# Two of nine tiles take their second expert table as one ordered pass and products with an on-chip weight matrix

## What is computed

```python
idx = jnp.take_along_axis(cidx, sel, axis=-1)      # cidx = i1 * 128 + i2
g = jax.nn.softmax(best, axis=-1)
ue = jnp.take(u, idx, axis=0)
ve = jnp.take(v, idx, axis=0)
a = jax.nn.gelu(jnp.einsum("thkd,td->thk", ue, tb), approximate=False)
return jnp.einsum("thk,thkd->td", g * a, ve)
```

## Time and profile before

| | before |
|---|---|
| median of 3 runs | 4154.73 us (4143.67 to 4164.61) |
| span of the profiled execution, first to last instruction | 4055.0 us |
| TensorE (PE) busy | 2755.5 us, 68% |
| VectorE (DVE) busy | 2362.3 us, 58% |
| GpSimd (POOL) busy | 2392.4 us, 59% |
| ScalarE (ACT) busy | 853.5 us, 21% |
| moved by DMA | 1373.95 MB, of it 1107.43 MB by the gathers |

### The profile page before, as it was taken

How to read it: one execution, slowest core, us unless ns; L and a number is a source line. 1 busy time by engine, 2 the same in 40 slices (tenths; PEclk the granted TensorE clock), 3 DMA queues, 4 the chain that set the end, 5 groups by cost and what they waited for, 6 DMA issues and landing times.

```text
span 4055.0 us, 39016 instructions
## 1 busy us (share of the span) xinstructions
PE 2755.5 (68%) x12071; PEld 1452.6 (36%) x12071; DVE 2362.3 (58%) x6192; ACT 853.5 (21%) x1884; POOL 2392.4 (59%) x2148
## 2 busy tenths in 40 slices
PE   8989987877789975568787888987453332333334
PEld 5667564534445432234444444443121000000000
DVE  2134356578865556646488886654566666666552
ACT  1235212244421110112144442111010000000000
POOL 1000034667756547756477776654777777777775
PEclk9989988977779987779877778998776665566556
DMA  6443387999999989989999999997999999999998
GB/s 219 124 142 101 139 285 268 389 359 385 390 349 394 386 336 375 395 312 387 356 387 361 385 394 394 381 374 289 368 391 388 381 370 367 385 387 366 382 369 345
DMA packets 540797, 1373.95 MB, mean 339 GB/s; under 512 B 50640, under 2 KB 246800, under 8 KB 540592
## 3 DMA queue, kind: packets, MB, share of 16 engines
q0 software_dynamic: 304128, 1107.43, 71.4%
q1 hardware_dynamic: 195040, 220.24, 16.2%
q10 hardware_dynamic: 41424, 43.80, 3.3%
HBM read 1319.26 MB, written 52.02 MB: 338 GB/s over the span
## 4 chain that ended last, share of the span: by engine, by line
PE 33%; POOL 25%; DMA 13%; DVE 11%; issue 10%; DVEq 3%; ACT 2%; SPq 1%; ACTq 1%; PEldq 0%; POOLq 0%; PEld 0%
POOL G_v_rows L713 13%; POOL G_u_rows L713 12%; PE scores L837 7%; DMA G_v_rows<-in_peer_v,G_idxT 5%; PE scores L1721 5%; PE y_sum L2226 4%; PE scores L1725 3%; DVE G_u_rows L2060 3%; PE scores L1915 3%; PE scores L1503 3%; PE scores L1810 2%; DMA scratch_dkT<-A_dkT 2%; PE scores L1410 2%; PE o L1445 1%; DMA D_w_br<-in_w_br_m 1%
## 5 line engine op out<-in xcount | busy, mean ns | idle before, releaser
L713 POOL DMA_INDIRECT G_u_rows<-in_peer_u,G_idx x1056 | 1199.9, 1136 | 756.7 <-issue 321.8
L2060 DVE CUSTOM_DVE_ANT_0 G_u_rows<-G_u_rows,G_h 128x1024 f32<-128x1024 f32 x1056 | 1274.7, 1221 | 431.2 <-DMA G_u_rows<-in_peer_u,G_idx 408.4
L713 POOL DMA_INDIRECT G_v_rows<-in_peer_v,G_idxT x1056 | 1177.9, 1115 | 486.9 <-issue 312.4
L2226 PE MATMUL y_sum<-G_v_rows,G_zw 128*32 128x512 f32 x4224 | 749.7, 846 | 877.1 <-DMA G_v_rows<-in_peer_v,G_idxT 853.0
L2226 PEld LDWEIGHTS y_sum<-G_v_rows,G_zw 128*32 128x32 f32 x4224 | 148.9, 137 | 1358.5 <-issue 1354.6
L837 PE MATMUL scores<-A_w_in,A_hT 128*128 128x256 f32 (+2 forms) x864 | 221.9, 417 | 22.9 <-DMA A_w_in<-in_w_in 15.5
L668 POOL MEMSET G_zw<- 128x1024 f32 x2 | 1.9, 963 | 395.9 <-SPq L630 395.9
L837 PEld LDWEIGHTS scores<-A_w_in,A_hT 128*128 128x128 f32 x864 | 168.7, 198 | 74.8 <-DMA A_w_in<-in_w_in 16.4
L1721 PE MATMUL scores<-D_hT,D_w_gate 128*128 128x384 f32 x512 | 172.9, 491 | 2.3 <-DMA D_w_br<-in_w_br_m 2.1
L1428 PE MATMUL turn<-ident,C_probs 128*128 128x128 f32 x635 | 133.4, 327 | 49.1 <-ACT C_pT L1536 41.2
L1960 DVE COPY F_sc<-scores 128x256 f32<-128x256 f32 (+1 forms) x72 | 29.3, 422 | 215.2 <-PE scores L1926 215.1
(11 more groups left out here) (282 smaller groups left out, 3940.7 us busy)
## 6 DMA issues: line engine op xcount, KB each, us to landing
A_w_in<-in_w_in SPq DMA_DIRECT2D x24, 1024.0 KB, 13.3
D_w_gate<-in_w_gate SPq DMA_DIRECT2D x24, 1024.0 KB, 22.9
G_u_rows<-in_peer_u,G_idx POOLq DMA_INDIRECT x1056, 7.8
G_v_rows<-in_peer_v,G_idxT POOLq DMA_INDIRECT x1056, 8.2
DF_w<-in_w_gate SPq DMA_DIRECT2D x12, 1024.0 KB, 21.0
DF_w<-in_peer_wq SPq DMA_DIRECT2D x12, 1024.0 KB, 10.3
F_w_q<-in_peer_wq SPq DMA_DIRECT2D x12, 1024.0 KB, 7.1
E_w_o<-in_w_o SPq DMA_DIRECT2D x18, 512.0 KB, 8.5
```

Of the source, the lines that this page charges most:

```text
L713: pool.indirect_dma_start(out=buf[:, :], out_offset=None, in_=table, in_offset=bass.IndirectOffsetOnAxis(ap=rows, axis=0)).then_inc(signal ...
L2060: dve.tensor_tensor_reduce(out=self.u_rows[slot][:, :], in0=self.u_rows[slot][:, :], in1=self.h2[t % 2][:, :], scale=1.0, scalar=0.0, op0= ...
L2226: last = pe.matmul(self.ps_y[32 * c:32 * (c + 1), cols], self.zw[b % 2][:, lo:lo + 32], self.v_rows[self.ring_v.slot[4 * quad + c]][:, col ...
```

## The change

For the token tiles 4 and 5 (places 5 and 6, steps 544 to 799) nothing is gathered from `peer_v`. The dots, ranks and gates stay as they are. Instead:

- The two key halves i1 and i2 and the weights of each pick are kept by token. When a tile is through, TensorE turns them to picks by tokens ("turn").
- For 8 tokens at a time ("build") VectorE compares the first halves with 64 numbers (512 elements), the second halves with 128 numbers (1024 elements), and multiplies the first result by the weights (512 elements). TensorE multiplies both for each token, which gives the token's weights by expert, and ScalarE copies them from PSUM into `spread_w`: 128 x 64 x 256 floats, for half of the experts and both tiles. There are 16 builds for each tile and half, 64 in all.
- SyncE, behind its dense work, reads `peer_v` from its first row to its last, two chunks of 128 rows (1 MB) for each load, into two buffers. For each of 128 chunks TensorE makes four products of 128 x 512 (two tiles, two halves of the columns) into PSUM.
- Half of the experts is streamed, then the weights of the other half are built over the first, then that half is streamed. By the constants: builds of half 0 in steps 737 to 833, chunks 0 to 63 from 835, builds of half 1 from 919, chunks 64 to 127 from 962 to 1046, the two sums and norms from 1048.
- The buffers lie over the dense ones and take the place of the additional ring slots; the rings stay at 8 and 10. POOL's wait for the end of the dense work goes. The chunks' PSUM is that of the scores.

The diff, cut to its core (`by_row` and `v_of` also renumber the second table's blocks and quads on every engine, `SUMMED` the sums; this isn't shown, nor are the norms' steps):

```diff
-SLOTS_U, SLOTS_V, MORE_U, MORE_V = 8, 10, 5, 4
+SLOTS_U, SLOTS_V = 8, 10
 GROUPS_ALL = KEY_TILES * HEADS + 2
 U_SLOTS = GROUPS_ALL * TOPK
+STREAMED = (5, 6)
+HALVES, CHUNKS, TOGETHER, CHUNK_SLOTS = 2, P, 8, 2
+KEYS_HALF = P // HALVES
+LAST_CHUNK = 1046
...
+SUMMED = [sum(a not in STREAMED for a in range(at)) for at in range(TILES + 1)]
+PASSED = (TOPK * FIRST[STREAMED[0]], TOPK * FIRST[STREAMED[-1] + 1])
+V_SLOTS = U_SLOTS - (PASSED[1] - PASSED[0])
+def by_row(step):
+    return not PASSED[0] <= step < PASSED[1]
+def v_of(step):
+    return step - max(0, min(step, PASSED[1]) - PASSED[0])
...
+        self.slot = [k % n for k in range(total)]
+        self.use = [k // n + 1 for k in range(total)]
+        self.prev = [k - n if k >= n else None for k in range(total)]
...
+        self.count = keep("count", [P, P])
+        self.ranks = self.count[:, 0:TOPK]
...
+    def stream_memory(self, ctx, sb):
+        n = len(STREAMED)
+        self.spread_w = sb(ctx, "T_spread_w", [P, KEYS_HALF, n * P])
+        self.chunks = [sb(ctx, f"T_chunks{i}", [P, 2, D]) for i in range(CHUNK_SLOTS)]
+        self.hot1 = [sb(ctx, f"T_hot1_{i}", [P, TOGETHER, KEYS_HALF]) for i in range(2)]
+        self.hot2 = [sb(ctx, f"T_hot2_{i}", [P, TOGETHER, P]) for i in range(2)]
+        self.picksT = [sb(ctx, f"T_picksT{i}", [P, 3, P]) for i in range(n)]
+        self.t_ms, self.t_root, self.t_rs = (sb(ctx, f"T_{x}", [P, n]) for x in ("ms", "root", "rs"))
+        self.keys_of = [self.g_q[:, 0:2 * P].rearrange("p (j k) -> p j k", k=P), self.dist[:, 0:2 * P].rearrange("p (j k) -> p j k", k=P)]
+        self.weights_of = [self.g_kv[:, 0:P], self.dist[:, 2 * P:3 * P]]
...
+    def stream_at(self):
+        dense = self.plan()[-1] - PRELUDE
+        ready = [max(dense, TOPK * FIRST[at + 1] + 1) + 1 for at in STREAMED]
+        units = P // TOGETHER
+        ticks = [(ready[0], ("turn", 0))]
+        for g in range(units):
+            ticks.append((ready[0] + 1 + g * (ready[1] - ready[0] - 2) // units, ("build", 0, 0, g)))
+        ticks.append((ready[1], ("turn", 1)))
+        for g in range(units):
+            ticks.append((ready[1] + 1 + 2 * g, ("build", 1, 0, g)))
+        start = ready[1] + 2 * units + 1
+        rest = [("chunk", c) for c in range(KEYS_HALF)]
+        rest += [("build", s, 1, g) for s in range(len(STREAMED)) for g in range(units)]
+        rest += [("chunk", c) for c in range(KEYS_HALF, CHUNKS)]
+        ticks += [(start + n * (LAST_CHUNK - start) // len(rest), tick) for n, tick in enumerate(rest)]
+        for s in range(len(STREAMED)):
+            ticks += [(LAST_CHUNK + 2 + 3 * s, ("sum", s)), (LAST_CHUNK + 4 + 3 * s, ("norm", s))]
...
-            if k == self.last_dense:
-                pool.wait_ge(self.opened, len(STAGES) + 1)
             if k < U_SLOTS:
                 self.gather_u(pool, k)
-            if k >= V_LAG:
-                self.gather_v(pool, k - V_LAG)
+            if k >= V_LAG and by_row(k - V_LAG):
+                self.gather_v(pool, v_of(k - V_LAG))
...
+            at, _, h = GROUP[m]
+            if at in STREAMED:
+                key = self.keys_of[STREAMED.index(at)][:, :, TOPK * h:TOPK * (h + 1)]
+                dve.tensor_reduce(key, hot[:, :, :].rearrange("p (j k) x -> p j k x", j=2), AX, ALU.add)
+            else:
+                key = self.key[:, :, :]
+                dve.tensor_reduce(key.rearrange("p j k -> p (j k)"), hot[:, :, :], AX, ALU.add)
...
+        if at in STREAMED:
+            own = self.weights_of[STREAMED.index(at)][:, TOPK * h:TOPK * (h + 1)]
+            last = dve.tensor_tensor(own, self.gelus[n % 2][:, :], self.gates[n % 4][:, :], ALU.mult)
+            if h == HEADS - 1:
+                last.then_inc(self.t_ready, 1)
+            return
...
+    def stream_sp(self, eng):
+        for c in range(0, CHUNKS, 2):
+            slot = c // 2 % CHUNK_SLOTS
+            if c >= 2 * CHUNK_SLOTS:
+                eng.wait_ge(self.t_streamed, c - 2 * CHUNK_SLOTS + 2)
+            rows = self.a["peer_v"][P * c:P * (c + 2), :].rearrange("(c p) n -> p c n", p=P)
+            eng.dma_start(self.chunks[slot][:, :, :], rows).then_inc(self.t_in[slot], 16)
+        eng.wait_ge(self.t_streamed, CHUNKS - 2 * CHUNK_SLOTS + 2)
+        for s, at in enumerate(STREAMED):
+            eng.dma_start(self.chunks[0][:, s, :], self.s["x1"][ORDER[at] * P:(ORDER[at] + 1) * P, :]).then_inc(self.t_in[0], 16)
+        for s, at in enumerate(STREAMED):
+            eng.wait_ge(self.t_finish, 3 * s + 3)
+            eng.dma_start(self.s["y"][P + ORDER[at] * P:P + (ORDER[at] + 1) * P, :], self.chunks[0][:, s, :]).then_inc(self.t_y, 16)
+        eng.wait_ge(self.t_y, 16 * len(STREAMED))
...
+    def stream_dve(self, dve, kind, *at):
+        tick = (kind,) + at
+        if kind == "build":
+            s, half, g = at
+            u = self.build_no[tick]
+            if u == 0:
+                dve.wait_ge(self.opened, len(STAGES) + 1)
+            if half == 0 and g == 0:
+                dve.wait_ge(self.t_turn_out, self.turn_no["turn", s] + 1)
+            if u >= 2:
+                dve.wait_ge(self.t_turned, self.turn_no[self.builds[u - 2]] + 1)
+            picks, lo = self.picksT[s], KEYS_HALF * half
+            toks = slice(TOGETHER * g, TOGETHER * (g + 1))
+            first, second = self.hot1[u % 2][:, :, :], self.hot2[u % 2][:, :, :]
+            def each(j, n):
+                return picks[:, j, toks].unsqueeze(2).to_broadcast([P, TOGETHER, n])
+            dve.tensor_tensor(first, self.count[:, lo:lo + KEYS_HALF].unsqueeze(1).to_broadcast([P, TOGETHER, KEYS_HALF]),
+                              each(0, KEYS_HALF), ALU.is_equal)
+            dve.tensor_tensor(second, self.count[:, :].unsqueeze(1).to_broadcast([P, TOGETHER, P]), each(1, P), ALU.is_equal)
+            dve.drain()
+            last = dve.tensor_tensor(first, first, each(2, KEYS_HALF), ALU.mult)
+            last.then_inc(self.t_hot, 1)
+        elif kind == "sum":
+            s, = at
+            x1, y = self.chunks[0][:, s, :], self.ps_s[s]
+            if s == 0:
+                dve.wait_ge(self.t_streamed, CHUNKS)
+                dve.wait_ge(self.t_in[0], 16 * (CHUNKS // 4 + len(STREAMED)))
+            dve.tensor_tensor(x1, y[:, :], x1, ALU.add)
+            dve.drain()
+            dve.tensor_tensor_reduce(out=y[:, :], in0=x1, in1=x1, scale=1.0 / D, scalar=EPS,
+                                     op0=ALU.mult, op1=ALU.add, accum_out=self.t_ms[:, s:s + 1])
+            dve.drain().then_inc(self.t_finish, 1)
...
+        if kind in ("turn", "build"):
+            n = self.turn_no[tick]
+            bank = self.ps_2[n % 2]
+            if n == 0:
+                pe.wait_ge(self.opened, len(STAGES) + 1)
+            if n >= 2:
+                pe.wait_ge(self.t_turn_out, n - 1)
+        if kind == "turn":
+            s, = at
+            pe.wait_ge(self.t_ready, s + 1)
+            for j, src in enumerate((self.keys_of[s][:, 0, :], self.keys_of[s][:, 1, :], self.weights_of[s])):
+                last = pe.transpose(bank[:, P * j:P * (j + 1)], src, self.ident[:, :])
+            last.then_inc(self.t_turned, 1)
+        elif kind == "build":
+            u = self.build_no[tick]
+            pe.wait_ge(self.t_hot, u + 1)
+            for i in range(TOGETHER):
+                last = pe.matmul(bank[:, KEYS_HALF * i:KEYS_HALF * (i + 1)], self.hot2[u % 2][:, i, :], self.hot1[u % 2][:, i, :],
+                                 start=True, stop=True)
+            last.then_inc(self.t_turned, 1)
+        elif kind == "chunk":
+            c, = at
+            half, i = divmod(c, KEYS_HALF)
+            slot = c // 2 % CHUNK_SLOTS
+            if i == 0:
+                pe.wait_ge(self.t_turn_out, self.built[half])
+            if c % 2 == 0:
+                pe.wait_ge(self.t_in[slot], 16 * (c // (2 * CHUNK_SLOTS) + 1))
+            for s in range(len(STREAMED)):
+                for cols in (slice(0, D // 2), slice(D // 2, D)):
+                    last = pe.matmul(self.ps_s[s][:, cols], self.spread_w[:, i, P * s:P * (s + 1)], self.chunks[slot][:, c % 2, cols],
+                                     start=(c == 0), stop=(c == CHUNKS - 1))
+            last.then_inc(self.t_streamed, 1)
...
+        if kind in ("turn", "build"):
+            n = self.turn_no[tick]
+            bank = self.ps_2[n % 2]
+            if n == 0:
+                act.wait_ge(self.opened, len(STAGES) + 1)
+            act.wait_ge(self.t_turned, n + 1)
+        if kind == "turn":
+            s, = at
+            act.activation(self.picksT[s][:, :, :].rearrange("p j n -> p (j n)"), bank[:, 0:3 * P], ACT.Copy).then_inc(self.t_turn_out, 1)
+        elif kind == "build":
+            s, half, g = at
+            if half and g == 0:
+                act.wait_ge(self.t_streamed, KEYS_HALF * half)
+            lo = P * s + TOGETHER * g
+            act.activation(self.spread_w[:, :, lo:lo + TOGETHER].rearrange("p i t -> p t i"),
```

(38 more changed lines are left out.)

77 lines of the change are left out of this document (41 added, 36 removed).

## The result

The changed kernel takes 4110.91 us in the median of 4 runs (4099.88 to 4118.80), the kernel before beside it 4150.96 us (4143.67 to 4164.61): a ratio of 0.9891, 95% interval 0.9862 to 0.9919. It is 1.1% faster where I forecast 2% slower, and 4111 lies under the range of 4140 to 4335.

The account below looks back on a forecast made before the run. The prediction took transfers to bound the kernel's end; its terms, -46 -76 -15 +161 +43 +10 +5 +5, summed to +87 us on 4154.7, so 4242 us, range 4140 to 4335.

Parts of the forecast that it names:

- So transfers bound the end: After the dense work, from 3088 us on: DMA share 0.99 to 1.00 at 378 GB/s taken as the bound.
- POOL never waits: From 3088 us on, POOL never waits for a buffer; nearly every gap before a gather is its own 0.3 us issue.
- The stream, +161: Steps 835 to 1046: 62.9 MB of table loads on an already full transfer queue, at 390 GB/s, cost 161 us.
- queueing: Product stretches: streamed products and quads of gathered rows, in order on TensorE, cost +10 us (0 to +60).
- rival 1: Transfer time is softer than its share says, so not slower: 4156 or 4098 us, steps near 3.5 us in products; chance 0.25.
- Score stage, -76: Steps 648 to 735: waits for second-table rows and queued scores go, VectorE bounds; 256 to 180 us (bounds -50 and -98).
- Merge and out, -46: Steps 584 to 648: removed products and shorter waits take the stage from 271 to 225 us (bounds -25 and -65).
- steps 735 to 840, -15: Behind the dense work: VectorE with 32 builds replaces transfers as bound; 277 us against 292 (bounds -35 and +5).
- build stretch, +43: Steps 919 to 962: VectorE needs 161 us for dots and 32 builds where 118 pass now (+25 to +60).
- the end, +10: Fewer ring slots +5 us; VectorE's wait before the two sums for last product and x1 +5 (each 0 to +15).
- about 100 us lie around the span: Whole kernel: profiled span 4055.0 us against a run median of 4154.7; the rest, launch and end, assumed to stay.
- Rival 2: Product stretches: TensorE becomes the bound, its products delaying quads and gathers; 4324 us, chance 0.17.

Follow-up runs that it names:

- half rows: Kernel before, with second-table gathers from step 792 on fetching 128 rows of 2 KB instead of 4 KB: 4096.26 us, ratio 1.0075.
- dots from PSUM: Kernel before, complete, with the dot's second input from step 752 on a copy of the token rows in PSUM: 4029.03 us, ratio 0.9905.

## Why the prediction was wrong

**The reading of the bound failed, and the largest miss follows from it.** The step was "So transfers bound the end". I took the DMA share of 0.99 to 1.00 at 378 GB/s for a full transfer queue. The runs with half rows and with dots from PSUM show that it was not; POOL's gathers, lengthened by VectorE's two-input dots, set the pace of 2.82 us. "POOL never waits" was the evidence for the bound on POOL, and I read it as evidence against.

**The stream, +161.** Forecast with queueing +171, measured +106. The sum added the stream's time to gathers at their old pace, as if transfers had set that pace. What holds is the bytes of both at the full rate: 163 steps x 1.049 MB + 62.9 MB = 234 MB, at the 412 GB/s of a 159 ns packet 568 us, measured 567, where the same steps took 461 before. The 10 us of queueing don't show beside that: with a quarter of the products the stretches kept their length. (84 x 2.82 + 81 is 318, not 319; nothing hangs on it.) The pace of the stretches was 3.5 us a step, as I had written for rival 1.

**Score stage, -76: right in kind, too small.** Measured -91. VectorE was busy 149.7 us, less than the 161 + 8 that 1.85 us a step made. My bound of 158 us for the stage was closer.

**Merge and out, -46 (measured -55); steps 735 to 840, -15 (-18); build stretch, +43 (+36); the end, +10 (+9).** All inside their bounds, and by the mechanisms that I gave: VectorE busy 258.9 of 271 us in steps 735 to 840 with 32 comparisons of 1219 ns, and a dip of the share in the build stretch. The share near 0.55 that I named for steps 735 to 840 was 0.69, at 230 GB/s: it doesn't follow the bytes. The rings cost 10 us at most, as priced. The clock rose with the stream, to 0.96 and more.

**The whole time.** That "about 100 us lie around the span" is false: it is under 2 us. By its span, the profiled execution came from a quicker kind of chip than the runs. This didn't shift the forecast of the difference, but it hid that the chips differ by 2%, more than the change. The touched stages explain 100 us between forecast and measurement on chip 9; on the chip of the result the whole is 127 us off (-40 for +87), and what lies between, outside these stages or in the chip, stays open.

**Rival 1** named what came out, by its signs: a score stage under 165 us (163) and over 390 GB/s in the product stretches (404 to 411). Its mechanism was only half right, since I put the softness down to the packets of scattered rows and limited it by POOL's 2.48 us, when POOL's 2.82 was the bound itself. So its numbers came out in part by luck. It should have been the forecast: two rows that I had shown, 409 GB/s in the last window and POOL's unbroken work, spoke for it. Rival 2 didn't come.

## What to carry to other kernels

A DMA share of 1.00 isn't a full queue. Compare its GB/s with the best window of the same packets, or with what their median time allows, and look at whether the engine that issues the gathers ever pauses for anything but its own issue: if it doesn't, it is likely the bound, and bytes on another queue are cheap until the full rate is reached. Where gathers are issued by GpSimd, keep one operand of VectorE's long two-input instructions in PSUM if banks are free; that was 1% here for three copies. Before moving work to an engine with idle time, look at its place in that engine's order: behind the waits of a chain it lengthened the chain, and the kernel by 3%.

## What the runs showed of the hardware

- A gather's instruction on POOL (128 rows of 4 KB) takes 0.94 us alone and beside one-input instructions of VectorE, and 1.07 to 1.15 us in the mean of a stretch full of dots with both inputs in SBUF; with one input in PSUM it is 0.945 us.
- One core moved 412 GB/s over 274 us, when an ordered pass on SyncE's queue ran beside two streams of gathers on POOL's. With the gathers alone it was 378 GB/s, and 400 once they weren't held up.
- A packet of 4096 bytes took 159 ns in the median of three stretches. Its mean was 162 ns where the rate was 411 GB/s, 171 at 378 and 195 at 230.
- The DMA share was 0.69 at 230 GB/s, 0.84 at 282, 1.00 at 378 and 1.02 at 412. It doesn't grow in proportion to the bytes.
- The same kernel took 4066 to 4073 us on chips 9 and 13, 4156 on chip 15 and 4151 on the chip of the result, with under 2 us around the span in every profiled run.
